# One core, a routed mixture of experts behind a token merge: routing the first four token tiles during the merge and running two full-width expert blocks while the rest are routed

## The reference, cut to what matters

```
h = modulate(rmsnorm(x, g), shift, scale)             # h2 in the kernel
logits = t @ w_router                                 # 16 experts in 4 groups
sel = softmax(logits) + b_router
best group = largest sum of its top two sel; idx = top 2 of sel inside it
w = p_sel / sum(p_sel)                                # gates
a, b = t @ wg[e], t @ wu[e]                           # 1024 -> 512 for each chosen expert
act = silu(a) * b * gate
out = x + gate2 * sum over experts of act @ wd[e]     # 512 -> 1024
```

## Time and profile before

| | |
|---|---|
| Time, 3 runs | median 1234.73 us, 1234.27 to 1238.36 |
| Profiled execution | span 1233.3 us; the page gives no other time of its own for it |
| PE busy | 1154.7 us (94%) |
| Busy DVE, ACT, POOL | 49%, 27%, 21% |
| Mean granted TensorE clock | 0.976 |
| DMA over the span | 253.37 MB, mean 205 GB/s |

### The profile page before, as it was taken

How to read it: one execution, slowest core, us unless ns; L and a number is a source line. 1 busy time by engine, 2 the same in 40 slices (tenths; PEclk the granted TensorE clock), 3 DMA queues, 4 the chain that set the end, 5 groups by cost and what they waited for, 6 DMA issues and landing times.

```text
span 1233.3 us, 19314 instructions
## 1 busy us (share of the span) xinstructions
PE 1154.7 (94%) x6769; PEld 540.8 (44%) x6769; DVE 600.7 (49%) x1161; ACT 336.7 (27%) x713; POOL 254.3 (21%) x312
## 2 busy tenths in 40 slices
PE   6999999999989899998999966999999999999996
PEld 4444444444446666665444433333333333333332
DVE  0010867786779999997965357111211211212212
ACT  2132221222138888887212221000000000000000
POOL 2011101221049600000100001123222222232322
PEclk9999999999999999999999986999999999999998
DMA  9843333322347465645833246996789878976663
GB/s 359 332 144 103 103 103 107 97 88 86 90 155 259 142 210 170 205 138 210 311 117 110 91 150 237 375 380 244 262 283 326 312 243 281 367 233 240 219 221 119
DMA packets 115859, 253.37 MB, mean 205 GB/s; under 512 B 15054, under 2 KB 29518, under 8 KB 114760
## 3 DMA queue, kind: packets, MB, share of 16 engines
q1 hardware_dynamic: 94241, 208.42, 48.6%
q0 software_dynamic: 17568, 39.35, 9.1%
q10 hardware_dynamic: 3984, 4.72, 1.1%
HBM read 399.77 MB, written 39.22 MB: 356 GB/s over the span
## 4 chain that ended last, share of the span: by engine, by line
PE 83%; DMA 5%; ACT 4%; issue 4%; DVE 3%; SPq 0%; ACTq 0%; POOL 0%; POOLq 0%; DVEq 0%
PE bank L1784 20%; PE bank L1461 20%; PE bank L1798 10%; PE bank L1652 8%; PE bank L1441 3%; PE bank L1495 2%; PE bank L1535 2%; PE bank L1545 2%; PE bank L1523 2%; PE bank L1774 2%; PE bank L1316 1%; DMA big<-in_w_up_dram 1%; DMA big<-in_w_down_dram 1%; PE bank L1558 1%; ACT mid L1123 1%
## 5 line engine op out<-in xcount | busy, mean ns | idle before, releaser
L1784 PE MATMUL bank<-big,mid 128*64 128x512 f32 x1232 | 283.1, 600 | 2.2 <-DMA big<-in_w_up_dram 1.7
L1461 PE MATMUL bank<-big 128*128 128x512 f32 x560 | 249.2, 598 | 0.1
L1461 PEld LDWEIGHTS bank<-big 128*128 128x128 f32 x560 | 103.7, 190 | 131.2 <-issue 131.2
L1784 PEld LDWEIGHTS bank<-big,mid 128*64 128x64 f32 x1232 | 87.1, 138 | 161.4 <-issue 160.5
L1957 DVE SCALAR_TENSOR_TENSOR cvT<-low,cw,cvT 128x256 f32<-128x256 f32 x360 | 156.9, 510 | 0.0
L1798 PE MATMUL bank<-big,mid 128*64 128x512 f32 x608 | 133.8, 592 | 1.2 <-DMA big<-in_w_down_dram 1.2
L2062 DVE TENSOR_TENSOR_SCAN big<-big 128x513 f32<-128x513 f32 (+4 forms) x96 | 90.2, 978 | 8.2 <-ACT big L1090 8.1
L2485 DVE TENSOR_TENSOR xt<-xt,bank 128x512 f32<-128x512 f32 x20 | 13.8, 688 | 148.5 <-ACT xt L1258 148.5
L2504 DVE TENSOR_TENSOR mid<-bank,low 128x512 f32<-128x512 f32 x38 | 24.5, 686 | 120.0 <-PE bank L1798 79.9
L1798 PEld LDWEIGHTS bank<-big,mid 128*64 128x64 f32 x608 | 44.0, 137 | 87.8 <-issue 87.8
L800 POOL TENSOR_TENSOR st<-st,mhalf 128x16 f32<-128x16 f32 (+1 forms) x9 | 25.2, 2801 | 252.6 <-DVE st L1988 243.9
(11 more groups left out here) (341 smaller groups left out, 1349.7 us busy)
## 6 DMA issues: line engine op xcount, KB each, us to landing
big<-in_w_gate_dram SPq DMA_DIRECT2D x42, 2048.0 KB
big<-in_w_up_dram SPq DMA_DIRECT2D x41, 2048.0 KB
big<-in_w_down_dram SPq DMA_DIRECT2D x41, 2048.0 KB
low<-in_w_ada_dram SPq DMA_DIRECT2D x32, 512.0 KB, 4.2
low<-in_cache_v_dram SPq DMA_DIRECT2D x64, 256.0 KB
big<-in_w_in_dram SPq DMA_DIRECT2D x8, 1280.0 KB, 17.1
xt<-in_x_prompt_dram SPq DMA_DIRECT2D x16, 512.0 KB, 4.7
mid<-in_w_ada_dram SPq DMA_DIRECT2D x8, 1024.0 KB, 13.9
```

Source lines behind the costliest of these rows:

```text
L1461: mm = pe.matmul(bank[:, 4 if cc == 2 else cc, :], hT[:, s, k, :], w_in_sb[:, k, cc * 512:(cc + 1) * 512], start=(k == 0), stop=(k == KD - 1))
L1784: mm = pe.matmul(bank[half, 2 * s + w, :], xgT[:, s, k, half], moving, start=(k == 0), stop=(k == KD - 1))
```

## The change

- DVE routes tiles 0 to 3 during merging (`early_logits`, `early_choice`), with the same operations as the later routing on 4 tiles in place of 9, picks the most used expert among their tokens (`early_expert`), places up to 256 of its pairs in two blocks of 128 slots (`early_places`) and finds their rows (`early_rows_of_slots`). PE adds `early_ranks` and `early_slots`.
- SP loads that expert's three matrices into slot 0, where those of expert 0 went before, once it is chosen. Expert 0's gate is loaded when both blocks' gates are done, its up when both blocks' ups are done, its down when both blocks' downs are done. The spare buffer is gone.
- POOL gathers the h2 rows of the blocks (`xe`), later their x1 rows, and scatters their results before the first pass's outputs are gathered.
- PE runs the two blocks (`early_turn`, `early_gate_or_up`, `early_turn_act`, `early_down`), with stationary operands of 128x128, in pieces between the last tiles of merging and the first pass. ACT and DVE do their sigmoid, products and residual.
- The pairs that the blocks took are subtracted in the rank counts (`shift_used`, `shift_gone`). Expert 15 then has 236 pairs left and 4 units, the sum is 36, `r_cut` is 18 and there are 18 passes. The lower half uses experts 0, 1, 2, 3, 3, 4, 4, 5, 5, 5, 6, 6, 6, 7, 8, 8, 9, 9 and the upper half 10, 10, 11, 12 six times, 13 twice, 14 three times, 15 four times. So pass 1 takes one new expert, passes 2 and 3 two each, passes 5, 7, 9, 10, 11 and 13 one, pass 14 two and pass 16 one.

```
# PE, in the loop over tiles
                 if t == NTP - 2:
+                    early_slots()
                     mix_sample()
...
+                if t + 2 == NTP - 1:
+                    mix(t + 2, 0, (0,))
+                    mix(t + 2, 0, (1,), (0, 2))
+                    early_ranks()
+                    mix(t + 2, 0, (1,), (2, 4))
...
                 if t == NTP - 1:
+                    early_gate_or_up(0, 0, 0, KD // 2)
                     row_sum()
...
+                if t == NTP - 2:
+                    early_turn(0)
+                    early_turn(1)
+                if t == NTP - 1:
+                    early_gate_or_up(0, 0, KD // 2, KD)
# PE, behind the loop
+            early_gate_or_up(1, 0, 0, KD)
+            early_gate_or_up(0, 1, 0, KD // 2)
             pe.wait_ge(S["mask_ready"], N0["mask_ready"] + 2)
...
+            early_gate_or_up(0, 1, KD // 2, KD)
+            early_gate_or_up(1, 1, 0, 6)
             pe.wait_ge(S["hot_ready"], N0["hot_ready"] + 1)
             to_slots(...)                       # rows of the first two passes
+            early_turn_act(0)
+            early_gate_or_up(1, 1, 6, KD)
+            early_down(0, 0)
+            early_turn_act(1)
+            early_down(0, 1)
+            pe.wait_ge(S["tok_ready"], 1)
+            early_down(1, 0)
+            early_down(1, 1)
# SP
+            def load_early_expert():
+                sp.wait_ge(S["pv_mm"], U)
+                sp.wait_ge(S["e_sel"], N0["e_sel"] + 1)
+                e = sp.value_load(early_exp[0:1, 0:1], min_val=0, max_val=E - 1)
+                for w_sb, w_d, landed in zip((wg_sb, wu_sb, wd_sb), (w_gate, w_up, w_down), e_w_in):
+                    sp.dma_start(w_sb[:, 0, :, :], ...).then_inc(landed, 16)
             for t in range(NT):
                 if t + 2 < NT:
                     load_x2(t + 2)
+                if t == NBT + 2:
+                    load_early_expert()
...
+            sp.wait_ge(S["e_gu"], N0["e_gu"] + NEB)
+            sp.dma_start(wg_sb[:, 0, :, :], w_gate[0, 0]...).then_inc(S["first_in"], 16)
             e0, = pass_experts(zero_exp, 0, 1)
+            sp.wait_ge(S["first_in"], N0["first_in"] + 16)
+            sp.wait_ge(S["e_gu"], N0["e_gu"] + 2 * NEB)
             load_w(wg_sb, w_gate, wg_in, e0, (0, None))
-            load_w(wu_sb, w_up, wu_in, e0, (0, None))
-            load_w(wd_sb, w_down, wd_in, e0, (0, None))
+            load_w(wu_sb, w_up, wu_in, e0, (None, None))
             sp.wait_ge(S["tiles_ready"], 2)
             e1, e2 = pass_experts(first_exp, 1, 2)
+            sp.wait_ge(S["e_y"], N0["e_y"] + 2 * NEB)
+            load_w(wd_sb, w_down, wd_in, e0, (None, None))
             sp.wait_ge(S["g_mm"], 1)
+            load_w(wg_sb, w_gate, wg_in, e1, e0)
# DVE, in the loop over tiles
                 normed(t)
+                if t == NBT + 1:
+                    early_expert()
+                if t == NBT + 2:
+                    early_rows_of_slots()
                 if t + 1 < NTP:
                     merged(t + 1)
+                if t == NBT + 1:
+                    early_places()
...
+                if t == NBT:
+                    early_logits()
+                    ln_swish(2)
+                    early_choice()
```

More of the change, by code:

```diff
@@ L1239, in _ @@
                 if t == LN_AT[2] + 1:
-                    nc.scalar.activation(st[:, 60:61], mhalf[:, 0:1], ACT.Exp)
+                    act.wait_ge(S["e_z"], N0["e_z"] + 1)
+                    nc.scalar.activation(b_e, b_z, ACT.Exp).then_inc(S["e_exp"], 1)
+                if t == NTP - 2:
+                    square(NTP - 1)
+                    for s in range(NEB):
+                        evac_xe(s)
+                    square(NTP)
             strip_logits(NT - 2)
@@ L1250, in _ @@
                 .then_inc(S["part_ready"], 1)
+            evac_acte(1)
             def turned_lo(s):
@@ L1712, in router_sum, with early_ranks @@
                     .then_inc(S["lg_mm"], 1)
+            def early_ranks():
+                pe.wait_ge(S["e_mask"], N0["e_mask"] + 1)
+                pe.wait_ge(S["ln_norm"], N0["ln_norm"] + 3)
+                ranks = bank[:, 7, 0:(NBT + 1) * E]
+                pe.matmul(ranks, before[:, :], b_maskb, start=True, stop=False)
+                for t in range(NBT):
+                    mm = pe.matmul(ranks[:, (t + 1) * E:].rearrange("p (t e) -> p t e", e=E), onesb[:, :],
+                                   b_maskb[:, t * E:(t + 1) * E].unsqueeze(1).broadcast_to([P, NBT - t, E]),
+                                   start=False, stop=(t == NBT - 1))
+                mm.then_inc(S["e_rank"], 1)
@@ new lines, in early_slots @@
+            def early_slots():
+                pe.wait_ge(S["e_hot"], N0["e_hot"] + 1)
+                for t in range(NBT):
+                    pe.matmul(bank[:, 7, 128:128 + 2 * NEB].rearrange("p (w n) -> p w n", w=2), b_at[:, t, :], b_id[:, t, :, :],
+                              start=(t == 0), stop=(t == NBT - 1))
+                pe.wait_ge(S["e_hot32"], N0["e_hot32"] + 1)
+                for t in range(NBT):
+                    mm = pe.matmul(bank[:, 7, 160:160 + NEB], b_at32[:, t, :], b_tw[:, t, :],
+                                   start=(t == 0), stop=(t == NBT - 1))
+                mm.then_inc(S["e_slots"], 1)
@@ new lines, in early_turn, with early_gate_or_up @@
+            def early_turn(s):
+                pe.wait_ge(xg_in[s], EARLY)
+                if s == 0:
+                    pe.wait_ge(S["x1_tmp"], N0["x1_tmp"] + NTP)
+                for k in range(KD):
+                    mm = pe.transpose(bank[:, XE_BANKS[s][k // 4], (k % 4) * P:(k % 4 + 1) * P],
+                                      xe[:, s, k * P:(k + 1) * P], identf[:, :])
+                mm.then_inc(S["e_xps"], 1)
+            def early_gate_or_up(s, w, k0, k1):
+                if w == 0 and k0 == 0:
+                    pe.wait_ge(S["e_xsb"], N0["e_xsb"] + 2 * s + 2)
+                if w == 1 and s == 1 and k0 == 0:
+                    pe.wait_ge(S["h2T_sb"], 2 * NT)
+                if k0 == 0:
+                    pe.wait_ge(e_w_in[w], E_W0 + 16)
+                for k in range(k0, k1):
+                    mm = pe.matmul(bank[:, (EG_BANK, EU_BANK)[w][s], :], xeT[:, s, k, :], (wg_sb, wu_sb)[w][:, 0, k, :],
+                                   start=(k == 0), stop=(k == KD - 1))
+                if k1 == KD:
+                    mm.then_inc(S["e_gu"], 1)
@@ new lines, in early_combine @@
+            def early_combine(s):
+                dve.wait_ge(S["e_y"], N0["e_y"] + 2 * s + 2)
+                dve.wait_ge(xb_in[s], EARLY)
+                dve.wait_ge(S["e_grow_in"], N0["e_grow_in"] + 16)
+                for h in range(2):
+                    half = slice(512 * h, 512 * (h + 1))
+                    c.put(V.tensor_tensor(ye[:, s, half], bank[:, EY_BANK[s] + h, :], gate_row[:, 0, half], ALU.mult))
+                c.wait()
+                V.tensor_tensor(ye[:, s, :], ye[:, s, :], xb[:, s, :], ALU.add).then_inc(S["e_done"], 1)
@@ L2322, in _ @@
                                AX_X, ALU.add))
+            for j in range(NEB):
+                early_swish(j)
             dve.wait_ge(S["rank_ready"], N0["rank_ready"] + 1)
@@ L2438, in _ @@
             dve.sem_inc(S["tiles_ready"], 1)
+            for j in range(NEB):
+                early_combine(j)
             def turned_hi(s):
```

315 lines of the change are left out of this document (259 added, 56 removed).

## The result

The changed kernel takes 1256.34 us (median of 4 runs, 1254.72 to 1257.9), the kernel before 1236.55 us beside it (4 runs, 1234.27 to 1239.88): a ratio of 1.0164, 95% interval 1.0142 to 1.0187. The prediction was 1243 us, in a range up to 1256; the measured time lies just above it. The direction and the places of the waits were right. What was too small are two terms of the sum, the waits for weights and the half clock behind them, by 13 us together.

The account below looks back on a forecast made before the run. PE was taken as the bound, idle or at half clock around routing, with DMA the second limit. 1233.3 + 30.6 - 1.3 - 45.1 + 23 + 6 - 5.7 + 2.3 = 1243.1, stated as 1243 us, range 1228 to 1256.

Parts of the forecast that it names:

- What is removed, and what the blocks cost: Pass loop and blocks: two passes of 22.56 us go, -45.1 us; the two blocks cost PE 45.0 us.
- Where the passes start, +30.6: Merging to first pass: the first gate starts at 792 instead of 761.4 us, ends 788 and 797.
- No PE wait over 2 us in routing: Routing, after merging: a sign given for the forecast, that PE has no wait longer than 2 us there.
- What the transfers do, +23 at passes 1 to 3: Weight waits of 4, 3.5, 3, 8.5, 4 us at gate(1), up(2), gate(3), down(2), up(3); ends 13 and 35.
- the walk: Passes 1 to 3: load-by-load count, each matrix asked for only when its buffer is free, giving 23 us of waits.
- Passes 13 and 14, +6: Pass 14 takes two new experts right behind pass 13's one: 6 us of waits, ends 2 and 12.
- The clock, -1.3 and +2.3: First gate's earlier half clock goes, -1.3 us; half clock behind new waits costs 4 us less 1.7 of before, +2.3.
- The rate: DMA engines in full stretches, from 760 us on: taken as 385 GB/s.
- Faster transfers: Rival: weight transfers at 408 GB/s, waits 9 us less, 1232 us, no change; chance 0.17.
- hidden weights: Rival: loads for passes 1 to 3 overlap, only waits like those of before remain, 1216 us; chance 0.14.
- The later start: Rival: blocks come later, gather and tile 6's stores queued behind weights, 5 to 12 us more, 1253 us; chance 0.13.

Follow-up runs that it names:

- free_after: The changed kernel without any weight load for passes 1 to 17, which multiply by stale weights: 1211.01 us.
- free_before: The kernel before without weight loads for passes 1 to 19 beyond those already loaded, so with stale weights: 1227.19 us.
- turn12_after: The changed kernel with the upper half beginning at another unit, so passes 3 and 14 no longer take two new experts: 1248.51 us, ratio 1.0119.
- kept_2: The changed kernel, halves exchanged, early expert kept for pass 0, other half's pass 0 up/down loaded early, no pass taking two new experts: 1229.0 us, ratio 0.9949.
- all_three: The changed kernel with earlier upper-half up/down loads, another upper-half order, and later early-expert loads, block turning and first gate: 1239.12 us, ratio 1.0042.
- slot1_after: The changed kernel with pass 0's upper-half up and down matrices loaded as soon as their expert is known: 1245.17 us, ratio 1.0078.
- kept_0: As kept_2 but with the upper half in plain order, so passes 7 and 13 take two new experts each: 1240.58 us, ratio 1.0048.

## Why the prediction was right, and where it was wrong

- **What is removed, and what the blocks cost.** Right. There are 18 passes, and `free_after` against `free_before` gives -16.2 us where the working has -45.1 and +29.
- **Where the passes start, +30.6.** Right: 790.70 instead of 792, with the wait for the gathered rows at the predicted place (4.95 us, predicted 5.7) and the end of merging at 749.3 (predicted 749). Of the 29.3 us, 1.9 are there before the change begins (the mix at 688.62 and 690.49 us), so the change itself adds 27.5, and the sum's 30.6 is 3 us high. (The terms given for the end of merging add to about 750, where the working has 749.) "No PE wait over 2 us in routing" held.
- **What the transfers do, +23 at passes 1 to 3.** The place of every wait was right, their size was not: they are 28.1 us, and with up(0) 29.2. The miss is at gate(1), which waits 12.66 instead of 4; the four waits behind it are 15.4 us instead of 19. Two things were missing in the walk. The first is bytes ahead of gate(1). From 773 to 820 us 17.9 MB went, where 385 GB/s from 771 to about 811 us, where the walk has gate(1) behind its 4 us, are 15.4. The queues of that stretch, plain transfers and then gathers and scatters, show which:

```profile
q1 hardware_dynamic: 5872, 13.93, 78.8%
q0 software_dynamic: 1281, 3.92, 22.1%
```

Six matrices, up to gate(1)'s, are 12.6 MB. The other 1.3 MB of q1 belong to up(1)'s matrix, which was asked for at 807.39 us while gate(1)'s was still on its way. Gathers and scatters took 3.9 MB. I had counted a pass's 2.1 MB evenly, but the scatters of both blocks, the first gathers of h2 rows and the gathers of pass 0 all fall into that stretch. The second thing is that a late gate(1) is not made good in full later: while it runs, none of the six buffers is free, and the engines move 0.8 MB from 820 to 830 us, nothing in the second half. My sum had them full until up(3). It had the bytes right, 47.1 MB against 45.3 from 771 to 902 us, but at 385 GB/s, and the mean was 346. SP's timeline shows the loads asked for around that hole:

```profile
798.20 0.81 SPq L768 DMA_DIRECT2D big<-in_w_gate_dram  x2
807.39 0.56 SPq L768 DMA_DIRECT2D big<-in_w_up_dram  x2
830.17 1.09 SPq L768 DMA_DIRECT2D big<-in_w_gate_dram  x2
836.80 0.55 SPq L768 DMA_DIRECT2D big<-in_w_down_dram  x2
```

- **Passes 13 and 14, +6.** 7.3 us. With the row above and the 5.7 of before, the waits are +30.8 where the sum has +23.3.
- **The clock, -1.3 and +2.3.** By what remains it is +6.4, 5.4 us more. I reckoned that where transfers set the pace a slower PE only waits less afterwards. That can hold only when the next thing waited for is already under way. It was behind the slow rows at 864.97 and 891.10: gate(3)'s matrix was asked for at 852.68 and up(3)'s at 875.12, and a faster PE would, by these rows, have waited some 4 us longer for them. It was not behind the one at 819.86, which ended in the freeing of the gate buffers, with the engines empty and the next load at 830.17, nor at 1157.13, where no wait follows. So about 4.5 of the 8.5 us are added time, and 4 could as well be counted to the waits; no run takes the clock away alone, and how the miss divides between the two terms stays an estimate.
- **The rate.** 378 to 394 GB/s in full stretches, as taken (385). The Trainium skill (DMA: Bandwidth & Descriptors, Bandwidth) gives 425 GB/s alone and about 358 as a share; these stretches lie between the two. The prediction's estimate by the second, 1255 us, is close to the measured time by luck: the mean of 346 GB/s from 771 to 902 us comes mostly from the hole at 820 to 830 us (8 us at 385 GB/s), not from a lower rate of full engines.
- **The rivals.** Faster transfers and hidden weights are out by the rate and by 36.5 us of waits. (At 408 GB/s the prediction's own sum gives a shortage of 20 us, not 18; that changes nothing here.) The later start is out, too. With 1253 us it has the time nearest to the measured one, but the start came where the forecast had it, so that would have been right for a wrong reason.

So the step that failed is the walk behind "+23": it spread the gathers evenly and kept the DMA engines full, and so had 4 us at gate(1) where 12.66 were measured, 6.2 us too little in all. With it failed the reasoning that a slow PE costs next to nothing there, 5.4 us too little; passes 13 and 14 add 1.3. The sum of the parts as measured, 1233.3 + 29.3 - 45.1 + 30.8 + 0.7 + 6.4 = 1255.4 us, is within 0.3 us of the span (the tail is 0.3 us shorter).

What stays open: why the times of `turn12_after`, `kept_2` and `all_three` scatter by 10, 11 and 19 us. The gathers of the late passes are the only waits that differ in kind, but there is one trace of each, so this is not shown.

## What to carry to other kernels

When a buffer gets a second user, its old contents have to be loaded at another time. Ask what was hidden there and what the DMA engines do at the new time: here 4.2 MB were worth about 11 us, wherever the wait then showed. With one buffer per operand, count bytes pass by pass, against what a pass carries (8.6 MB in 22.56 us at 381 GB/s): the two experts of pass 14 cost 9.7 us (7.3 of waits, 2.4 of half clock), and spreading such pairs over the passes won 11.6 us at the same bytes. A wait for a transfer can cost more than its length: PE ran at half clock behind the long ones, and behind the longest the DMA engines stood idle while the late matrix was used and no buffer came free.

## What the runs showed of the hardware that was not expected

SP's own issue of a load can last long. In the changed kernel it took up to 12.44 us when several matrices were on their way, and what stands behind it on SP was issued only afterwards. The DMA engines were full meanwhile (share 1.00 from 830 to 900 us), so no transfer time is seen lost by it:

```profile
852.68 8.44 SPq L768 DMA_DIRECT2D big<-in_w_gate_dram  x2
861.39 8.03 SPq L768 DMA_DIRECT2D big<-in_w_down_dram  x2
875.12 12.44 SPq L768 DMA_DIRECT2D big<-in_w_up_dram  x2
```

In `kept_2`, with four matrices less in all and never more than one expert in a pass, the issues from 766 to 850 us took 0.08 to 0.90 us. In merging, behind the early expert's three matrices, the issues of tile 6's two stores took 4.12 and 1.80 us, and tile 8's normed waited 2.63 us for the second; that was off the path.

The clock fell to 0.50 also behind short waits: half a gate took 5.29 us instead of 3.65 behind 3.30 us and 5.35 behind 2.22 (`slot1_after`), and 5.35 behind 2.05 us in `kept_0` at 957.11 (its clock from 959 to 961 us is 0.50), while behind 2.02 us in the changed kernel it took 3.65.
